# Gate weights loaded behind the fifth weight unit, gate rows read back behind the next unit, memory values stored two units later

## The chip, the cores and the metric

The kernel runs on one core of one Trainium2 chip. The metric is device microseconds of one execution of the whole program. The compared number is the median of the runs; the profile is one further execution.

## What is computed

The reference is one layer of a hybrid streaming encoder for 256 prompt tokens and 64 sample tokens (320 tokens, width 1024). Cut to what matters here:

```python
k = (rmsnorm(mem) @ w_mem_k); v = (rmsnorm(mem) @ w_mem_v)     # outputs mem_k_prompt, mem_v_prompt
z = rmsnorm(x) @ w_in                                          # 15 projections side by side
ig, lf = i_raw + i_b, log_sigmoid(f_raw + f_b)                 # the gates: 4 + 4 columns of w_in
bcum = cumsum(lf); m = max(...)                                # row maxima, outputs mlstm_m
w_intra = exp(dmat - m); w_inter = exp(inter - m)              # weights of the mLSTM heads
att = softmax(mq @ k.T) @ v                                    # attention into the memory tokens
x = x + (sum of three gated branches) @ w_out
x = x + hier_moe(rmsnorm(x))                                   # 32 experts, all weights streamed
```

All matrix products use a split of each float32 operand into a rounded high part and a rest, and three products of the parts.

## The kernel before, in words

The work is a list of steps, made once (`make_steps`), and every engine walks the list and does its own part of each step. The dense weights are cut into units of 1 MB, numbered from 0 in the order in which TensorE uses them: 0 to 3 are `w_mem_k`, 4 to 7 `w_mem_v` (each half of the contraction), 8 to 11 the query of the memory attention (`mq`), 12 to 19 the mLSTM queries and keys (`qk`), and so on. A unit goes through four hands:

1. SyncE (SP) issues its load (L711) into one of two raw slots (a third serves unit 2). From unit 3 on it waits first until VectorE has finished with the unit that held the slot (L707, semaphore `u_lo`): unit 3 waits for the rest of unit 0, unit 4 for that of unit 1, and unit n from 5 on for that of unit n-2.
2. ScalarE makes the high part (`unit_first_part`, L1228), after TensorE is done with the unit that held the rounded slot.
3. VectorE makes the rest (`unit_second_part`, L1634) and counts `u_lo`.
4. TensorE multiplies (L892 for `memk`, L827 for `memv`, L793 for `mq`, `qk` and others), after waiting for `u_lo`.

SP is one queue: what stands between two unit loads in the program delays the second. All its transfers run on the same 16 DMA engines. Before the change SP issues, around the places touched:

- ahead of unit 3: the three tiles of x (L702), then `load_gate_weights` (L618 to L625): two transfers of four columns of `w_in` each (1024 rows, 16 bytes of a row), two bias columns and the start maxima `m0c`. TensorE needs them for the step `gates`, which follows the first `memv` step of unit 4.
- behind unit 10: `spread_gate_rows` (L633 to L638) waits for the last exponential of the gate rows (`s_g4`), writes four rows to DRAM (L636), waits for that write (`s_rbw`), and reads them back, broadcast to 128 partitions (L638, 770 KB). VectorE waits for the read-back at its first `bc` step (L1733 to L1735).
- behind unit 11: `store_memory` (L640 to L648) stores the two `mlstm_m` outputs and then four halves of `mem_k_prompt` and `mem_v_prompt`.
- behind unit 13: a wait for all four of those stores, then the read of the prompt keys out of `mem_k_prompt` (L603, L610).

The order of steps at the read-back is `mq 0, bc 0, mq 1, (unit 10: high part and rest), bc 1, mq 2, ...`. Engine by engine: ScalarE evacuates `mq 0`, takes the exponential of `bc 0` (L1311, after VectorE's sum with the read-back rows), evacuates `mq 1` (L1321), and only then makes the high part of unit 10. VectorE does `bc 0`, then the rest of unit 10. TensorE does `mq 0` to `mq 3` from units 8 and 9 and then waits for unit 10.

The space of `memk` and `memv` is reused at the step `attention_done` (L1353, L1782, L2128), where three engines wait for all four stores.

Of the kernel before, what the change touches and what calls it, by code (L numbers as in the profile page):

```python
# [226 lines left out]
def unit_slot(n):  # L227

    return n if n < 3 else (n - 1) % RING
# [11 lines left out]
def build_kernel(nc, ins, outs):  # L241
    I, O = ins, outs
    ctx = ExitStack()
    with ctx:
# [3 lines left out]
        def sem(name):  # L248
            return ctx.enter_context(nc.semaphore(name))
# [56 lines left out]
        def take(*dims):  # L306
            v = at(off[0], *dims)
            off[0] += int(np.prod(dims))
            return v
# [9 lines left out]
        memk = take(2, D)  # L319
        memv = take(2, D)  # L320
# [148 lines left out]
        s_memout, s_cvout, s_cvs = sem("mem_out"), sem("conv_out"), sem("conv_rows")  # L469
# [44 lines left out]
        def done(*name):  # L514

            s = _by_name[name]
            return freed[s["ring"], s["eng"]], s["evacuated"]
# [29 lines left out]
        def _(sp):  # L547
            for r0, name in ((P_MIX, "norm_mix_g"), (P_MEM, "mem_norm_g")):
                sp.dma_start(prows[r0:r0 + 8, :], I[name][0, :].rearrange("(c p) -> c p", p=128)).then_inc(s_gains, 16)
            for i in range(2):  # L550
                sp.dma_start(mem_tm[:, i, :], I["mem_prompt"][0, i * 128:(i + 1) * 128, :]).then_inc(s_mem[i], 16)
                src = I["w_mem_k"][0, i * (D // 2):(i + 1) * (D // 2), 0:256].rearrange("(k p) n -> p k n", p=128)
# [48 lines left out]
            def load_key_blocks(dst, keys, signal):  # L601
                for a in range(4):
                    sp.dma_start(dst[32 * a:32 * a + 32, :].rearrange("i (b d) -> i b d", d=64),  # L603
                                 keys.rearrange("(b i) (a d) -> a i b d", i=32, d=64)[a]).then_inc(signal, 16)

            def load_cached_keys(h):
                load_key_blocks(cmk[:, h % 2, :], I["cache_mem_k"][0, 0, :, h, :], s_keys[h % 2])

            def load_prompt_keys(h):
                load_key_blocks(memk_b[:, h, :], O["mem_k_prompt"][0, 0, :, h, :], s_keys[h % 2])  # L610

            def load_cache_v(h):
                sp.dma_start(cmv[:, h % 2, :, :], I["cache_mem_v"][0, 0, :, h, :].rearrange("(j p) d -> p j d", p=128)).then_inc(s_cachev[h % 2], 16)

            def load_state(h):
                sp.dma_start(C0[:, h % 2, :, 0:HD], I["state_mlstm_C"][0, 0, h].rearrange("(k p) e -> p k e", p=128)).then_inc(s_c0[h % 2], 16)

            def load_gate_weights():  # L618

                sp.wait_ge(s_const, 3)  # L620
                for c0, col in ((0, I0), (32, F0)):
                    sp.dma_start(wif[:, :, c0:c0 + H], I["w_in"][0, :, col:col + H].rearrange("(k p) n -> p k n", p=128)).then_inc(s_par, 16)
                sp.dma_start(ib[:, :], I["mlstm_i_b"][0, :].rearrange("(h a) -> h a", a=1)).then_inc(s_par, 16)
                sp.dma_start(fb[:, :], I["mlstm_f_b"][0, :].rearrange("(h a) -> h a", a=1)).then_inc(s_par, 16)
                sp.dma_start(m0c[:, :], I["state_mlstm_m"][0, 0, :].rearrange("(h a) -> h a", a=1)).then_inc(s_par, 16)  # L625
            def load_router():
                sp.dma_start(bsb[:, :, :], I["gmlp_b_s"][0].partition_broadcast(128)).then_inc(s_bs, 16)
                sp.dma_start(wr[:, :, 0:G], I["w_router_group"][0].rearrange("(k p) n -> p k n", p=128)).then_inc(s_par3, 16)
                sp.dma_start(wr[:, :, G:G + E], I["w_router_expert"][0].rearrange("(k p) n -> p k n", p=128)).then_inc(s_par3, 16)
                sp.dma_start(wrb[:, 0:G], I["b_router_group"][0, :].partition_broadcast(128)).then_inc(s_par3, 16)  # L630
                sp.dma_start(wrb[:, G:G + E], I["b_router_expert"][0, :].partition_broadcast(128)).then_inc(s_par3, 16)

            def spread_gate_rows():  # L633

                sp.wait_ge(s_g4, 1)
                sp.dma_start(spread_rows, rb[0:H, :]).then_inc(s_rbw, 16)  # L636
                sp.wait_ge(s_rbw, 16)
                sp.dma_start(rbb[:, :, :].rearrange("p h t -> p (h t)"), spread_rows.rearrange("h t -> (h t)").partition_broadcast(128)).then_inc(s_rbb, 16)  # L638

            def store_memory():  # L640

                sp.wait_ge(s_g3, 1)
                sp.dma_start(O["mlstm_m_prompt"][0, 0, :].rearrange("(h a) -> h a", a=1), rows[0:H, R_MM, TP - 1:TP]).then_inc(s_mout, 16)
                sp.dma_start(O["mlstm_m_sample"][0, 0, :].rearrange("(h a) -> h a", a=1), rows[0:H, R_MM, T - 1:T]).then_inc(s_mout, 16)
                sp.wait_ge(*done("memv", 1, 1, 1))
                for name, src in (("mem_k_prompt", memk), ("mem_v_prompt", memv)):
                    for i in range(2):
                        sp.dma_start(O[name][0, 0, i * 128:(i + 1) * 128].rearrange("p h d -> p (h d)"), src[:, i, :]).then_inc(s_memout, 16)  # L648

            def store_conv():  # L650

                sp.wait_ge(*done("cvT", 1))
                for i, name in enumerate(("mlstm_conv_prompt", "mlstm_conv_sample")):
                    sp.dma_start(O[name][0, 0].rearrange("j (c p) -> (j c) p", p=128), cvs[:, i, :]).then_inc(s_cvout, 16)

            def keep_keys(h):

                sp.wait_ge(*done("kt", h, 0))
                sp.dma_start(k_store[:, h, :], kw[:, 0:2, :].rearrange("p i d -> p (i d)")).then_inc(s_kst, 16)
# [38 lines left out]
            for n, (name, col, *part) in enumerate(UNITS):  # L698
                if n == 3:
                    for i, (t0, rows_) in enumerate(TILES):  # L700
                        src = I["x_prompt"][0, t0:t0 + rows_, :] if i < 2 else I["x_sample"][0, :, :]
                        sp.dma_start(x_tm[0:rows_, i, :], src).then_inc(s_x, 16)  # L702
                    load_gate_weights()
                if n == 0:
                    continue
                if n >= 3:
                    sp.wait_ge(u_lo, n - 2 if n < 5 else n - 1)  # L707
                w = 512 if part else 256
                r0 = part[0] * 512 if part else 0
                src = I[name][0, r0:r0 + UW // w * 128, col:col + w].rearrange("(k p) n -> p k n", p=128)  # L710
                sp.dma_start(raw_unit[unit_slot(n)].rearrange("p (k n) -> p k n", n=w), src).then_inc(unit_full[unit_slot(n)], 16)  # L711
                if n == 6:
                    sp.dma_start(ws[:, :, :], I["gmlp_w_s"][0].rearrange("g t s -> t g s")).then_inc(s_ws, 16)
                elif n in (8, 9):
                    load_cached_keys(n - 8)
                    load_cache_v(n - 8)
                elif n == 10:
                    spread_gate_rows()
                elif n == 11:
                    store_memory()  # L720
                elif n == 13:
                    sp.wait_ge(s_memout, 64)
                    load_prompt_keys(0)
                    load_prompt_keys(1)
                elif n in (16, 18):
                    sp.wait_ge(s_kmT, n - 14)
                    load_cached_keys(n // 2 - 6)
                    load_prompt_keys(n // 2 - 6)
                elif n in (19, 21):
                    sp.wait_ge(*done("av", (n - 19) // 2, 1))  # L730
                    load_cache_v((n - 15) // 2)
                elif n == 23:
                    sp.wait_ge(*done("av", 3, 1))
                    load_state(0)
                    load_state(1)
                elif n == 24:
                    load_router()
                elif n == 26:
                    store_conv()
                elif n == 28:  # L740
                    keep_keys(0)
                    keep_values()
                elif n in (30, 33, 37, 40):
                    h = (30, 33, 37, 40).index(n)
                    store_state(h)
                    if h < 2:
                        load_state(h + 2)
                elif n in (31, 34, 38):
                    keep_keys((31, 34, 38).index(n) + 1)
                elif n == 43:  # L750
                    store_normalizer()
                elif n == 47:
                    store_gating_values()
                if n == len(UNITS) - 9:
                    load_unit(0, 0)
                elif n == len(UNITS) - 3:
                    load_unit(0, 1)
# [1482 lines left out]
```

## Time and profile before

| | |
|---|---|
| median of 3 runs | 840.59 us (840.16 to 841.1) |
| profiled execution | 841.19 us |
| its span in the trace | 839.4 us, 12162 instructions |
| TensorE busy | 823.4 us, 98% |
| VectorE, ScalarE, GpSimd busy | 586.7, 469.1, 62.8 us |
| DMA | 191.83 MB, mean 229 GB/s |
| granted TensorE clock | 0.998 |

The views used below are the page, the waits (who waited for whom, in total), the timeline (instructions in order of time, equal ones merged, with the idle time before the first of them in brackets and what ended it), the DMA issues (with the time from issue to landing), and windows of one microsecond each. "SPq" rows are issues of DMAs by SyncE; the second number is how long the issue took SyncE, not how long the transfer ran. A merged row that holds several issues spans the waits between them.

### The profile page before, as it was taken

The page shows a single profiled execution, that of the slowest core. Times are in us where ns is not written, and L with a number is a line of the kernel's source. Part 1 is how long each engine was busy: PE and PEld are TensorE (multiplying, and loading weights), DVE is VectorE, ACT ScalarE, POOL GpSimd, SP SyncE. Part 2 cuts the span into 40 slices and gives each one's busy share as a digit, 9 for nine tenths or more (in the row PEclk, how much of TensorE's full clock was granted, in tenths as well). Part 3 has the DMA queues.
Part 4 walks back from the last instruction along what each step waited for, and adds up shares of the span by engine and source line. Part 5 has one row for each costly group of instructions (what it writes and reads, how often), then busy time and mean ns, then how long its engine had stood idle before and what let it go on. Part 6 is the DMA issues. An engine that isn't in the chain of part 4 may idle for free. (4 is left out here: it accounts for less than half of the span.)

```text
span 839.4 us, 12162 instructions
## 1 busy us (share of the span) xinstructions
PE 823.4 (98%) x4744; PEld 732.3 (87%) x4744; DVE 586.7 (70%) x820; ACT 469.1 (56%) x622; POOL 62.8 (7%) x113
## 2 busy tenths in 40 slices
PE   7999999999999999999999999999999999999995
PEld 7979989988989998899999999878888888888884
DVE  5665487773445456695565456778989889889894
ACT  5645577754333324554333336656877768767773
POOL 1000100010000000000000000020004102210410
PEclk9999999999999999999999999999999999999999
DMA  8659855327534536345436467589999999999970
GB/s 269 208 142 291 221 142 132 118 81 220 165 126 126 176 115 199 126 151 163 152 110 216 151 201 256 209 264 409 389 357 351 358 397 381 352 373 366 382 279 18
DMA packets 111841, 191.83 MB, mean 229 GB/s; under 512 B 18692, under 2 KB 76960, under 8 KB 111648
## 3 DMA queue, kind: packets, MB, share of 16 engines
q1 hardware_dynamic: 109824, 185.91, 65.0%
q0 software_dynamic: 1152, 3.41, 1.1%
q10 hardware_dynamic: 800, 1.66, 0.6%
q8 instruction: 40, 0.66, 0.3%
q14 instruction: 25, 0.20, 0.1%
HBM read 181.70 MB, written 10.03 MB: 228 GB/s over the span
## 5 line engine op out<-in xcount | busy, mean ns | idle before, releaser
L1643 DVE TENSOR_TENSOR w_r<-arena,w_r 128x2048 fp32r<-128x2048 f32 x96 | 217.0, 2286 | 27.6 <-ACT w_r L1239 27.6
L1634 DVE TENSOR_TENSOR unit_r<-arena,unit_r 128x2048 fp32r<-128x2048 f32 x63 | 144.3, 2291 | 131.2 <-ACT unit_r L1228 131.1
L793 PE MATMUL pj<-xn_r,unit_r 128*128 128x320 f32 x1536 | 233.2, 311 | 0.8 <-issue 0.8
L793 PEld LDWEIGHTS pj<-xn_r,unit_r 128*128 128x128 f32 x1536 | 225.6, 188 | 4.7 <-issue 3.7
L1130 PE MATMUL pj<-w_r,xg 128*128 128x512 f32 x768 | 191.0, 398 | 0.5 <-DVE xg L1627 0.4
L1239 ACT ACTIVATE w_r<-arena 128x2048 fp32r<-128x2048 f32 x96 | 180.3, 1909 | 2.7 <-DMA arena<-in_w_exp_down 2.0
L1130 PEld LDWEIGHTS pj<-w_r,xg 128*128 128x128 f32 x768 | 141.8, 188 | 31.5 <-DVE xg L1627 0.8
L1228 ACT ACTIVATE unit_r<-arena 128x2048 fp32r<-128x2048 f32 x63 | 120.9, 1919 | 44.4 <-PE pj L793 23.6
L1159 PE MATMUL pj<-w_r,hidT 128*128 128x512 f32 x384 | 93.3, 392 | 0.6 <-ACT hidT L1490 0.6
L1159 PEld LDWEIGHTS pj<-w_r,hidT 128*128 128x128 f32 x384 | 71.8, 188 | 17.0 <-issue 0.8
L793 PE MATMUL pj<-br_r,unit_r 128*128 128x320 f32 x384 | 59.6, 311 | 0.0
L793 PEld LDWEIGHTS pj<-br_r,unit_r 128*128 128x128 f32 x384 | 56.7, 188 | 1.1 <-issue 1.1
L1490 ACT ACTIVATE hidT<-ms 128x256 fp32r<-128x256 f32 x32 | 12.3, 385 | 70.6 <-PE ms L1140 70.6
L827 PE MATMUL pj<-unit_r,xn_r 128*128 128x512 f32 x192 | 46.2, 394 | 0.0
L827 PEld LDWEIGHTS pj<-unit_r,xn_r 128*128 128x128 f32 x192 | 35.4, 188 | 7.7 <-issue 0.3
L1381 ACT ACTIVATE arena<-pj 128x320 f32<-128x320 f32 x24 | 10.4, 433 | 33.0 <-PE pj L793 33.0
L793 PE MATMUL pj<-u_r,unit_r 128*128 128x320 f32 x192 | 28.8, 309 | 0.0
L1650 DVE SCALAR_TENSOR_TENSOR arena<-arena,prT 128x323 f32<-128x323 f32 x48 | 27.3, 570 | 1.7
L793 PEld LDWEIGHTS pj<-u_r,unit_r 128*128 128x128 f32 x192 | 28.3, 188 | 0.0
L892 PE MATMUL pj<-unit_r,mn_r 128*128 128x256 f32 x192 | 24.3, 285 | 2.8 <-DVE unit_r L1638 1.7
L892 PEld LDWEIGHTS pj<-unit_r,mn_r 128*128 128x128 f32 x192 | 23.4, 191 | 3.4 <-issue 2.1
L915 PE MATMUL pj<-unit_r,mix_r 128*128 128x256 f32 x192 | 24.1, 283 | 0.1
(344 smaller groups left out, 793.3 us busy)
## 6 DMA issues: line engine op xcount, KB each, us to landing
arena<-in_w_in SPq DMA_DIRECT2D x40, 1024.0 KB, 5.5
arena<-in_w_exp_gate SPq DMA_DIRECT2D x64, 512.0 KB, 4.9
arena<-in_w_exp_up SPq DMA_DIRECT2D x64, 512.0 KB, 6.7
arena<-in_w_exp_down SPq DMA_DIRECT2D x64, 512.0 KB, 5.6
arena<-in_w_mem_v SPq DMA_DIRECT2D x4, 1024.0 KB, 5.3
arena<-in_w_br_mem SPq DMA_DIRECT2D x4, 1024.0 KB, 5.1
arena<-in_w_br_mlstm SPq DMA_DIRECT2D x4, 1024.0 KB, 5.1
arena<-in_w_br_gmlp SPq DMA_DIRECT2D x4, 1024.0 KB, 4.9
```

The lines of the kernel that those rows point to most:

```text
L793: last = mm(bank_of(s)[0:out_rows, 0:out_cols], l, r, start=k == 0, stop=k == len(pairs) - 1)
L827: last = mm(bank_of(s)[0:rows_, 0:512], l, r, start=kh + k + m == 0, stop=kh == 1 and k == 3 and m == passes - 1)
L892: last = mm(b[:, 0:256], mn_r[:, p, k, a[1] * 128:a[1] * 128 + 128], w[:, q, k, :], start=k + m == 0, stop=k == KC - 1 and m == 2)
L915: last = mm(b[0:n, 0:256], mix_r[:, p, k, t0:t0 + n], w[:, q, k, :], start=k + m == 0, stop=k == KC - 1 and m == 2)
L1130: last = mm(pj[:, x % 2, :].rearrange("p (h n) -> p h n", h=2), xg[g % 2][:, k0 + k, xp, :], w[:, wp, k, :, :], start=k0 + j == 0, stop=k0 ...
L1159: last = mm(pj[:, 2 + half, :], hidT[:, x % 2, xp, c, :], w_r[u % NS][:, wp, c * D + half * 512:c * D + half * 512 + 512], start=e == 0 an ...
L1228: af(unit_part(n, 0), raw_columns(n), ACT.Copy).then_inc(u_hi, 1)
L1239: af(w_r[u % NS][:, 0, :], raw_w[u % NS], ACT.Copy).then_inc(m_hi, 1)
L1490: af(hidT[:, x % 2, 0, :, :].rearrange("p a b -> p (a b)"), ms[:, x % 2, 0:DE], ACT.Copy).then_inc(m_hth, 1)
L1634: v.tensor_tensor(unit_part(n, 1), raw_columns(n), unit_part(n, 0), ALU.subtract).then_inc(u_lo, 1)
L1643: v.tensor_tensor(w_r[u % NS][:, 1, :], raw_w[u % NS], w_r[u % NS][:, 0, :], ALU.subtract).then_inc(m_lo, 1)
L1650: ins = v.scalar_tensor_tensor(o, r[:, j:j + CONVW], prT[:, P_CW + 16 * j + c:P_CW + 16 * j + c + 1], o, ALU.mult, ALU.add)
```

## The change

Three moves on SP's list; no computation changes.

- `load_gate_weights` goes from ahead of unit 3 to behind unit 4.
- The write of the gate rows stays behind unit 10; the wait for it and the read-back go behind unit 11. The stores of `mem_k_prompt` follow the read-back.
- The two `mlstm_m` stores go behind unit 12, the stores of `mem_v_prompt` behind unit 14. The read of the prompt keys behind unit 13 waits for the two key stores alone.

```diff
-            def spread_gate_rows():
+            def write_gate_rows():
                 sp.wait_ge(s_g4, 1)
                 sp.dma_start(spread_rows, rb[0:H, :]).then_inc(s_rbw, 16)
+            def spread_gate_rows():
                 sp.wait_ge(s_rbw, 16)
                 sp.dma_start(rbb[:, :, :].rearrange("p h t -> p (h t)"), spread_rows.rearrange("h t -> (h t)").partition_broadcast(128)).then_inc(s_rbb, 16)
...
-                    load_gate_weights()
                 if n == 0:
                     continue
...
-                if n == 6:
+                if n == 4:
+                    load_gate_weights()
+                elif n == 6:
...
                 elif n == 10:
+                    write_gate_rows()
+                elif n == 11:
                     spread_gate_rows()
-                elif n == 11:
-                    store_memory()
+                    store_memory("mem_k_prompt", memk)
+                elif n == 12:
+                    store_maxima()
                 elif n == 13:
-                    sp.wait_ge(s_memout, 64)
+                    sp.wait_ge(s_memout, 32)
                     load_prompt_keys(0)
                     load_prompt_keys(1)
+                elif n == 14:
+                    store_memory("mem_v_prompt", memv)
```

## Rows read from the trace of the kernel before

**Rows 1.** The page: busy time of engines.

```profile
PE 823.4 (98%) x4744; PEld 732.3 (87%) x4744; DVE 586.7 (70%) x820; ACT 469.1 (56%) x622; POOL 62.8 (7%) x113
```

**Rows 2.** Waits of TensorE, whole span: total us, times, longest.

```profile
PE pj L892 <- DVE unit_r L1634: 1.0, 1, 1.0
...
PE pj L793 <- issue: 0.8, 1, 0.8
```

**Rows 3.** Timeline, 0 to 70 us: start, duration (us), engine, line, operation.

```profile
11.86 4.52 SPq L622 DMA_DIRECT2D arena<-in_w_in  x2
12.26 1.22 DVE L1638 TENSOR_TENSOR unit_r<-arena,unit_r 128x1024 fp32r<-128x1024 f32 x1
...
21.62 1.06 ACT L1274 ACTIVATE arena<-arena 128x1024 f32<-128x1024 f32 x1 [0.68 <-DMA arena<-in_x_sample]
21.81 0.39 SPq L711 DMA_DIRECT2D arena<-in_w_mem_k  x1
...
24.67 0.19 ACT L1274 ACTIVATION_READ_ACCUMULATOR arena<-arena 64x1 f32 x1
...
26.87 1.91 ACT L1228 ACTIVATE unit_r<-arena 128x2048 fp32r<-128x2048 f32 x1 [2.01 <-DMA arena<-in_w_mem_k]
...
28.81 2.29 DVE L1634 TENSOR_TENSOR unit_r<-arena,unit_r 128x2048 fp32r<-128x2048 f32 x1 [3.57 <-ACT unit_r L1228]
...
31.25 3.11 PE L892 MATMUL pj<-unit_r,mn_r 128*128 128x256 f32 x24 [1.04 <-DVE unit_r L1634]
...
34.54 2.29 DVE L1634 TENSOR_TENSOR unit_r<-arena,unit_r 128x2048 fp32r<-128x2048 f32 x1
...
39.55 3.05 PE L827 MATMUL pj<-unit_r,mn_r 128*128 128x512 f32 x12
```

**Rows 4.** Windows of 1 us: engines, clock, DMA busy share, GB/s.

```profile
17.00:18.00 1.00, 1.00 (x10) 1.00 (x10) 0.99 (x2) 0.66 (x2) 0.00 (x0) 1.00 1.08 422
...
21.00:22.00 1.00, 1.00 (x11) 1.00 (x10) 1.00 (x1) 0.38 (x1) 0.00 (x0) 1.00 0.08 2
```

**Rows 5.** DMA issues near 22 us (units 3 and 4): KB, us to landing.

```profile
arena<-in_w_mem_k SPq DMA_DIRECT2D x1, 1024.0 KB, 5.0
arena<-in_w_mem_v SPq DMA_DIRECT2D x1, 1024.0 KB, 7.3
```

**Rows 6.** Timeline, 67 to 140 us, around the read-back.

```profile
69.70 2.29 DVE L1634 TENSOR_TENSOR unit_r<-arena,unit_r 128x2048 fp32r<-128x2048 f32 x1 [2.18 <-ACT unit_r L1228]
...
72.14 0.34 SPq L638 DMA_DIRECT2D arena<-gate_rows  x1
...
72.52 0.43 SPq L711 DMA_DIRECT2D arena<-in_w_in  x1
...
76.29 0.35 DVE L1735 TENSOR_SCALAR arena<-arena,cols 128x256 f32<-128x256 f32 x1 [3.30 <-DMA arena<-gate_rows]
...
77.93 2.06 ACT L1228 ACTIVATE unit_r<-arena 128x2048 fp32r<-128x2048 f32 x1
80.03 2.29 DVE L1634 TENSOR_TENSOR unit_r<-arena,unit_r 128x2048 fp32r<-128x2048 f32 x1 [2.86 <-ACT unit_r L1228]
...
82.42 21.35 PE L793 MATMUL pj<-xn_r,unit_r 128*128 128x320 f32 x144 [0.82 <-issue]
```

**Rows 7.** DMA issues at 66.8 us (unit 10), 72.1 us (read-back), 72.5 us (unit 11).

```profile
arena<-in_w_in SPq DMA_DIRECT2D x1, 1024.0 KB, 5.2
...
arena<-gate_rows SPq DMA_DIRECT2D x1, 770.0 KB, 4.1
...
arena<-in_w_in SPq DMA_DIRECT2D x1, 1024.0 KB, 8.2
```

**Rows 8.** Timeline, later: where unit 11 and unit 14 are first used, unit 14's issue.

```profile
84.74 2.06 ACT L1228 ACTIVATE unit_r<-arena 128x2048 fp32r<-128x2048 f32 x1
...
95.25 17.33 SPq L711 DMA_DIRECT2D arena<-in_w_in  x3
...
107.69 1.91 ACT L1228 ACTIVATE unit_r<-arena 128x2048 fp32r<-128x2048 f32 x1
```

More of the change, by code:

```diff
@@ L631, in load_router, with store_maxima @@
                 sp.dma_start(wrb[:, G:G + E], I["b_router_expert"][0, :].partition_broadcast(128)).then_inc(s_par3, 16)
-            def spread_gate_rows():
+            def write_gate_rows():
                 sp.wait_ge(s_g4, 1)
                 sp.dma_start(spread_rows, rb[0:H, :]).then_inc(s_rbw, 16)
+            def spread_gate_rows():
                 sp.wait_ge(s_rbw, 16)
                 sp.dma_start(rbb[:, :, :].rearrange("p h t -> p (h t)"), spread_rows.rearrange("h t -> (h t)").partition_broadcast(128)).then_inc(s_rbb, 16)
-            def store_memory():
+            def store_maxima():
                 sp.wait_ge(s_g3, 1)
@@ L644, in store_memory @@
                 sp.dma_start(O["mlstm_m_sample"][0, 0, :].rearrange("(h a) -> h a", a=1), rows[0:H, R_MM, T - 1:T]).then_inc(s_mout, 16)
+            def store_memory(name, src):
                 sp.wait_ge(*done("memv", 1, 1, 1))
-                for name, src in (("mem_k_prompt", memk), ("mem_v_prompt", memv)):
-                    for i in range(2):
-                        sp.dma_start(O[name][0, 0, i * 128:(i + 1) * 128].rearrange("p h d -> p (h d)"), src[:, i, :]).then_inc(s_memout, 16)
+                for i in range(2):
+                    sp.dma_start(O[name][0, 0, i * 128:(i + 1) * 128].rearrange("p h d -> p (h d)"), src[:, i, :]).then_inc(s_memout, 16)
             def store_conv():
```

## The prediction

> **What bounds the kernel now.** I read the page first. TensorE is busy for 98% of the span and the next engine for 70% [rows 1], so in the end only time in which TensorE stands still, or starts standing still, counts. VectorE, ScalarE and the DMA engines matter where TensorE waits for them. So the second view is the list of TensorE's own waits. Two of its entries concern the places that the change touches: 1.0 us at the first multiplication of unit 3, ended by VectorE's rest, and 0.8 us in the projection at L793, put down to "issue" [rows 2]. Everything else that the change moves lies beside running matmuls. The third view is the timeline around these two gaps, which says what was really late.
>
> *First gap, at 31.25 us* [rows 3]. TensorE could have gone on at 31.25 - 1.04 = 30.21 us. Read it backwards: VectorE's rest of unit 3 ran from 28.81 to 31.10, ScalarE's high part from 26.87, and that one had waited 2.01 us for the load. The load was issued at 21.81, although its slot was free at 12.26 + 1.22 = 13.48. In between SP was issuing the gate weights and small columns, from 11.86 on. In that time the DMA engines ran dry: full at 17 to 18 us (422 GB/s), idle at 21 to 22 us (2 GB/s) [rows 4]. So SP's queue, not bandwidth, made unit 3 late.
>
> *Second gap, at 82.42 us* [rows 6]. TensorE could have gone on at 81.60. VectorE's rest of unit 10 ended at 80.03 + 2.29 = 82.32. It had waited for ScalarE (77.93 on), and ScalarE came to unit 10 only behind the first `bc` step, which VectorE began at 76.29 after 3.30 us of waiting for the read-back of the gate rows. The read-back was issued at 72.14 and took 4.1 us [rows 7]. So here the chain is: read-back landed, 76.29; then 6.1 us of VectorE, ScalarE, ScalarE, VectorE in a fixed order; then TensorE. Any delay of the read-back is a delay of TensorE, one for one, because 0.82 us of stall is already there. That is the main point of this forecast.
>
> **Part 1, gate weights behind unit 4.** Removed from ahead of unit 3: five issues, from 11.86 to 21.81. Unit 3 is now issued at about 13.5, right behind x in the queue. What does it cost to transfer? Units 3 and 4 were issued at 21.81 and 22.25 and landed 5.0 and 7.3 us later [rows 3, 5], at 26.81 and 29.55: a megabyte behind a megabyte adds 2.74 us (unit 4's issue is the next thing SP does, 0.44 us later). Behind x, which landed no later than 21.62, unit 3 therefore lands by 24.4. ScalarE is busy with the squares of x until 24.67 + 0.19 = 24.86, so it starts the high part there or earlier, not at 26.87: a gain of 2.0 us for VectorE, which ends at about 29.1. TensorE needs it at 30.21. The stall of 1.04 us goes whole, with 1.1 us to spare. If the transfer turned out up to 1.1 us slower, nothing changes; if x and unit 3 shared the bandwidth so badly that it was 2 us slower, the gain would be near zero. What is late next: unit 4's rest, at 34.54 + 2.29 = 36.83, used at 39.55 [rows 3], 2.7 us of room, so a shift of 1.04 is covered.
>
> The five issues now stand behind unit 4's load, whose slot is free once the rest of unit 1 is done, so they start at about 18 us. They took 9.95 us before (11.86 to 21.81), so SP is free at about 28.5. Queued behind them is unit 5, which must wait for the rest of unit 3 (29.1 in the new run) anyway. The gate weights themselves are needed behind the first step of `memv`, 39.55 + 3.05 - 1.04 = 41.6 us. They have some 13 us of cover; without it the cost would be the 10 us of issue. I take -1.04, with bounds -1.2 and 0.
>
> **Part 2, the read-back behind unit 11.** SP issued the read-back at 72.14 and unit 11 at 72.52. Unit 11's own condition, the rest of unit 9, was met at 69.70 + 2.29 = 71.99 [rows 6]. In the changed kernel unit 11 goes out at 72.0 and the read-back at about 72.4: SP's wait for the write ends at about the same moment as before, so its removal from in front of unit 11 is worth 0.5 us to a load that ScalarE takes up only at 84.74, 12 us later [rows 8]. That gain is nil on TensorE's path.
>
> The cost is the read-back's place in the queue. It now has 1 MB in front of it. By units 3 and 4 a transfer issued just behind another one lands later by its own size at the same rate: 2.74 us per 1024 KB, so 770 KB add 2.06. Unit 11 would land at 72.0 + 5.2 (unit 10's time [rows 7]) = 77.2, and the read-back at 79.3. Before it was there at 76.24. So it is 3.0 us late. Bounds: a lower one is 2.4, if the queue moves at the 422 GB/s of [rows 4] (1.05 MB / 422 GB/s = 2.5, with unit 11 0.15 us ahead of the old read-back). The upper one comes from unit 11 itself, which took 8.2 us behind the read-back and in front of the stores, landing at 80.7, 4.5 us after it instead of 2.7 [rows 7]. The two key stores now follow the read-back at once, and if they slow it in that proportion, 770 KB take 3.4 and it lands at 80.6, 4.4 us late. I take 3.0, since the sum by units 3 and 4 is two loads in a row, as here, and the stores are behind it.
>
> The Trainium skill, DMA: Bandwidth & Descriptors, "Anatomy of one DMA", gives a fixed part of about 2 us and bytes over 436 GB/s for the rest. By it the megabyte ahead would cost an estimated 2.4 us and not 3.0, and the whole change would come out 0.6 us better than below, at 842.0. The trace's own step from unit 3 to unit 4, 2.74 us per megabyte [rows 5], is slower than that, and the sum goes by the trace.
>
> TensorE's stall at `mq 4` grows from 0.82 to 3.8 us: all of the delay goes through, as shown above. What follows is ordered by TensorE again: unit 11's parts wait for `mq` to free slots, unit 12's load waits for the rest of unit 11. None of it is nearer to an absolute time, so nothing is won back.
>
> **Part 3, stores.** `mlstm_m` (two issues) behind unit 12, `mem_v_prompt` (two issues, 1 MB) behind unit 14, the wait for stores at unit 13 now for two. Behind unit 14 (issued at 95.25, taken up by ScalarE at 107.69 [rows 8]) some 3 us of stores in the queue fit into the room even if they delayed that unit wholly. Their finish is needed only at the end of attention, far behind. Their going away from 74 to 77 us relieves unit 11, which had 4 us of room already (landed 80.7, used 84.74). I cost this part at 0, with bounds -0.3 and +0.3.
>
> **Sum.** -1.04 + 3.0 + 0 = +2.0 us. The profiled execution took 841.19 and would take 843.2; it lies 0.6 above the median of the runs. Against the median, 840.59 + 2.0 = 842.6. Its own bounds: 840.59 - 1.2 + 2.4 - 0.3 = 841.5, and 840.59 + 0 + 4.4 + 0.3 = 845.3 if every part goes badly.
>
> **Rivals.**
>
> *A. The read-back is not held up by the unit in front* (0.20). If the engines work on both transfers at once, the later and smaller one may land nearly as early: delay 0 to 1, total 839.6 to 840.6, not slower. The place is the DMA queue at 72 us, and the point from which it decides is a delay of 1.04 us, where both parts cancel. For it speaks that the transfers are issued only 0.4 us apart. Against it speaks that unit 4, issued 0.44 us behind unit 3, landed 2.74 us behind it [rows 5], and that before the change unit 11, 0.38 us behind the read-back, did not keep it from landing in 4.1 us.
>
> *B. TensorE's clock falls in the longer gap* (0.12). The gap grows from 0.82 to 3.8 us; the granted clock reads 1.00 in every window read here, the 2.4 GHz level [rows 4], and no gap of such a length is in the trace. If TensorE came back at 1.2 GHz, 320 columns would take 267 ns each. Now 24 such matmuls take 21.35 / 6 = 3.56 us, 148 ns each [rows 6]. So a group of 24 costs 2.8 us more. Half a group to a whole one: 844.0 to 845.4. The Trainium skill, TensorE: Matmul & The Clock Gate, "Part 1: The HAM clock gate", says that an idle array falls to half its clock and regains it after sustained work; the trace of before has no row to weigh that against.
>
> *C. Unit 3 lands no earlier in use* (0.08). Then only part 2 counts: 843.6. Against it stands the idle stretch of the DMA engines at 21 us [rows 4].
>
> *D. The order makes no difference* (0.05): both stalls stay as they are, 840.6. *E. A gain from the stores that I don't see* (0.05): under 838.9.
>
> **How the numbers follow.** The main case has 0.50, with 842.6 and 841.5 to 845.3. Predicted is 842.6. The range 839.7 to 845.0 takes in the main case, C, D, nearly all of A and half of B, and leaves out about 1 in 8. The cases on both sides of no change hold most of the chance, so the main case's own range stands above. A measurement of this kernel can tell about 0.2% from no change, 1.7 us: faster means under 838.9, slower over 842.3. Slower: four fifths of the main case, since most of its span lies above 842.3 (0.40), B 0.12 and C 0.08: 0.60. Faster: E and a tenth of A, 0.07. Same: the rest, 0.33.
>
> **What the profile of the changed kernel would show.** For part 1: unit 3's load issued near 13.5 us, no TensorE wait at L892 for L1634, the DMA engines not idle at 21 us, and the gate weights issued between 18 and 28 us. For part 2: the read-back's issue directly behind unit 11's, its landing time well above 4.1 us (6.9 by the sum), VectorE's wait for `gate_rows` near 6.3 us instead of 3.3, and TensorE's gap before `mq 4` near 3.8 us. For part 3: unit 14's high part without a wait for its load. B would show a granted clock under 1.00 behind that gap. The forecast is wrong if the read-back lands within 5 us of its issue, or if `mq 4` starts less than 1 us later, after the shift of part 1, than it did.

## The result and the profile after

The changed kernel takes 845.9 us (median of 6 runs, 845.73 to 847.08); the kernel before, run beside it, 840.85 (840.05 to 842.34). The ratio is 1.0061, 95% interval 1.0048 to 1.0074. It is slower, as forecast, but by 5.05 us and not by 2.0, and it lies outside the range. Below, medians are set against those of the kernel before in the same comparison, which were 840.25 to 840.59 in the later ones.

The page of the changed kernel, engines and clock, to be laid beside [rows 1]. The fifth slice of the clock line reads 8:

```profile
PE 825.9 (98%) x4744; PEld 735.3 (87%) x4744; DVE 586.8 (70%) x820; ACT 469.3 (56%) x622; POOL 62.6 (7%) x113
...
PEclk9999899999999999999999999999999999999998
```

TensorE's waits, against [rows 2]. The wait at unit 3 (L892 for L1634 before, L904 for L1646 now) is gone, and what is left at L904 is for another line; the one "by issue" at the projection (L793 before, L805 now) has gone from 0.8 to 4.8 us:

```profile
PE pj L805 <- issue: 4.8, 1, 4.8
PE pj L904 <- DVE unit_r L1650: 1.8, 2, 1.3
```

The timeline at the front, against [rows 3]. Unit 3 is issued at 13.36, ScalarE comes from the squares of x straight to its high part, and the gate weights are issued from 18.07 on:

```profile
13.36 0.39 SPq L716 DMA_DIRECT2D arena<-in_w_mem_k  x1
...
18.07 4.70 SPq L622 DMA_DIRECT2D arena<-in_w_in  x2
...
24.41 0.19 ACT L1286 ACTIVATION_READ_ACCUMULATOR arena<-arena 64x1 f32 x1
24.51 1.90 ACT L1240 ACTIVATE unit_r<-arena 128x2048 fp32r<-128x2048 f32 x1
...
26.43 2.29 DVE L1646 TENSOR_TENSOR unit_r<-arena,unit_r 128x2048 fp32r<-128x2048 f32 x1 [1.44 <-ACT unit_r L1240]
```

The timeline at the read-back, against [rows 6]:

```profile
65.78 14.34 PE L805 MATMUL pj<-xn_r,unit_r 128*128 128x320 f32 x96
...
70.43 0.37 SPq L716 DMA_DIRECT2D arena<-in_w_in  x1
...
70.84 0.58 SPq L642 DMA_DIRECT2D arena<-gate_rows  x1
71.47 1.07 SPq L654 DMA_DIRECT2D out_mem_k_prompt<-arena  x2
78.89 0.35 DVE L1747 TENSOR_SCALAR arena<-arena,cols 128x256 f32<-128x256 f32 x1 [7.48 <-DMA arena<-gate_rows]
...
80.52 2.01 ACT L1240 ACTIVATE unit_r<-arena 128x2048 fp32r<-128x2048 f32 x1
82.56 2.29 DVE L1646 TENSOR_TENSOR unit_r<-arena,unit_r 128x2048 fp32r<-128x2048 f32 x1 [2.81 <-ACT unit_r L1240]
...
84.95 23.60 PE L805 MATMUL pj<-xn_r,unit_r 128*128 128x320 f32 x144 [4.83 <-issue]
```

The chain is the one of before, step for step: read-back, VectorE, ScalarE, VectorE, TensorE. The read-back landed 7.9 us after its issue (DMA issues, against [rows 7], where it took 4.1):

```profile
out_mem_k_prompt<-arena SPq DMA_DIRECT2D x2, 512.0 KB, 9.8
arena<-gate_rows SPq DMA_DIRECT2D x1, 770.0 KB, 7.9
```

The fifth `mq` step starts at 84.95 and not at 82.42, 2.5 us later. That is the gap's growth of 4.0 us less 1.5 us by which TensorE came to it earlier (80.12 and not 81.60).

The last line of the timeline shows the second loss: 144 matmuls took 23.60 us, where the same 144 took 21.35 [rows 6]. The windows of 1 us (engines' busy time, then granted clock, DMA share, GB/s) say why:

```profile
80.00:81.00 1.00, 0.12 (x1) 0.00 (x0) 0.00 (x0) 1.00 (x4) 0.64 (x3) 1.00 0.24 86
...
83.00:84.00 1.00, 0.00 (x0) 0.00 (x0) 1.00 (x1) 0.00 (x0) 0.00 (x0) 0.55 0.00 0
...
86.00:87.00 1.00, 1.00 (x6) 1.00 (x5) 0.41 (x4) 1.00 (x6) 0.73 (x3) 0.50 0.80 180
...
89.00:90.00 1.00, 1.00 (x6) 1.00 (x5) 0.61 (x1) 0.35 (x1) 0.00 (x0) 0.54 0.35 117
90.00:91.00 1.00, 1.00 (x9) 1.00 (x8) 1.00 (x1) 0.00 (x0) 0.00 (x0) 1.00 0.00 0
```

TensorE's last matmul ended at 80.12. The clock fell from 2.4 to 1.2 GHz about 3 us later, and TensorE came back at 84.95 to half speed, 5 or 6 matmuls in a microsecond instead of 9, until close to 90 us.

### The profile page after: what moved, and what is told of

Its sections match the earlier page's. It is cut to its first block, busy times and chain, and to the rows that moved or that the text cites. A ratio compares the mean times of both kernels' runs of the same rounds, so it can differ in the third digit from the quotient of the medians.

```text
span 843.9 us, 12162 instructions
## 1 busy us (share of the span) xinstructions
PE 825.9 (98%) x4744; PEld 735.3 (87%) x4744; DVE 586.8 (70%) x820; ACT 469.3 (56%) x622; POOL 62.6 (7%) x113
## 4 chain that ended last, share of the span: by engine, by line
PE 93%; DVE 2%; DMA 2%; ACT 2%; issue 1%; POOL 0%; SPq 0%; POOLq 0%; DVEq 0%; ACTq 0%
PE pj L805 36%; PE pj L1142 21%; PE pj L1171 10%; PE pj L839 8%; PE pj L927 3%; PE pj L904 3%; PE ms L973 1%; PE ms L992 1%; PE pj L846 1%; DMA arena<-gate_rows 1%; DMA arena<-in_w_in 1%; PE ms L1152 1%; PE ms L1008 1%; ACT unit_r L1240 1%; PE ms L861 1%
## 5 line engine op out<-in xcount | busy, mean ns | idle before, releaser
L805 PE MATMUL pj<-xn_r,unit_r 128*128 128x320 f32 x1536 | 235.5, 313 | 4.8 <-issue 4.8
L805 PEld LDWEIGHTS pj<-xn_r,unit_r 128*128 128x128 f32 x1536 | 227.8, 190 | 8.8 <-issue 7.7
L1646 DVE TENSOR_TENSOR unit_r<-arena,unit_r 128x2048 fp32r<-128x2048 f32 x63 | 144.3, 2290 | 130.7 <-ACT unit_r L1240 130.7
L805 PE MATMUL pj<-br_r,unit_r 128*128 128x320 f32 x384 | 59.6, 311 | 0.0
L805 PEld LDWEIGHTS pj<-br_r,unit_r 128*128 128x128 f32 x384 | 56.7, 188 | 1.1 <-issue 1.1
L805 PE MATMUL pj<-u_r,unit_r 128*128 128x320 f32 x192 | 28.8, 309 | 0.0
L805 PEld LDWEIGHTS pj<-u_r,unit_r 128*128 128x128 f32 x192 | 28.3, 188 | 0.0
L904 PE MATMUL pj<-unit_r,mn_r 128*128 128x256 f32 x192 | 24.1, 285 | 1.8 <-DVE unit_r L1650 1.8
L904 PEld LDWEIGHTS pj<-unit_r,mn_r 128*128 128x128 f32 x192 | 23.3, 191 | 2.3 <-issue 2.2
```

The costliest lines, as they stand in the source:

```text
L805: last = mm(bank_of(s)[0:out_rows, 0:out_cols], l, r, start=k == 0, stop=k == len(pairs) - 1)
L904: last = mm(b[:, 0:256], mn_r[:, p, k, a[1] * 128:a[1] * 128 + 128], w[:, q, k, :], start=k + m == 0, stop=k == KC - 1 and m == 2)
L1646: v.tensor_tensor(unit_part(n, 1), raw_columns(n), unit_part(n, 0), ALU.subtract).then_inc(u_lo, 1)
```

## The experiments

Theory: the whole loss is the read-back's place in the queue, paid twice, once as a longer gap and once as half a clock. The main rival is that the other two moves cost something too, or that the two losses aren't what they seem.

**Undo part 2 only.** The read-back is again directly behind its write:

```diff
                     write_gate_rows()
-                elif n == 11:
                     spread_gate_rows()
+                elif n == 11:
                     store_memory("mem_k_prompt", memk)
```

> The changed kernel with the read-back of the gate rows put back directly behind its write, ahead of unit 11; gate weights behind unit 4 and the later stores stay. Theory (the whole loss is the read-back's place: 4.0 us of delay and 2.25 us of halved clock): TensorE's gap before the fifth mq step is 0.8 us again, the clock stays at 1.00, and the time is 1.2 to 1.5 us under the kernel before, about 839.5. Rival (the gate weights' new place or the stores also cost something): at or above the kernel before, 840.9 or more.

Measured: 839.85 us, ratio 0.9995 (0.9986 to 1.0004). The gap is 0.9 us, the clock 1.00. The whole loss of the change goes with this one move. The gain against the kernel before is only 0.4 us and not told from nothing; 1.2 to 1.5 were expected. TensorE's waits of this kernel:

```profile
PE pj L805 <- issue: 0.9, 1, 0.9
```

**Undo part 1 only.** `load_gate_weights` back ahead of unit 3:

```diff
                         sp.dma_start(x_tm[0:rows_, i, :], src).then_inc(s_x, 16)
+                    load_gate_weights()
...
-                if n == 4:
-                    load_gate_weights()
-                elif n == 6:
+                if n == 6:
```

> The changed kernel with the gate weights back ahead of unit 3; only the read-back's place and the stores are changed against the kernel before. Theory: the two parts are independent, so this is the changed kernel plus the 1.2 to 1.5 us that the front gave: 847.2, with the wait of 1.0 us at unit 3 back and the gap of 4.8 us and the half clock as they are. Rival (moving the gate weights is what lengthened the wait for the read-back): clearly under the changed kernel's 845.9.

Measured: 845.9 us, ratio 1.0062 (1.0048 to 1.0075), no worse than the changed kernel. The read-back took 8.2 us, the gap was 5.0 us, and the clock fell. Here the theory missed as the forecast did: the wait at unit 3 did not come back. The timeline of this kernel's SP shows the unit out at 20.33, not at 21.81:

```profile
11.63 4.15 SPq L622 DMA_DIRECT2D arena<-in_w_in  x2
15.83 3.79 SPq L623 DMA_DIRECT2D ib<-in_mlstm_i_b  x1
...
20.33 0.67 SPq L717 DMA_DIRECT2D arena<-in_w_mem_k  x1
```

The same issues took 9.95 us of SP in the profiled execution of the kernel before and 8.7 here, for the same work. TensorE's stretch from the first to the second of these rows is 9.10 us, against 10.20 in the kernel before (the third and fourth row) and 8.93 in the changed one (23.81 to 32.74):

```profile
23.91 0.27 PE L950 MATMUL ms<-ident,arena 56*128 56x56 f32 x1
...
33.01 1.04 PE L932 MATMUL ms<-ident,arena 128*128 128x128 f32 x8
```

```profile
24.00 0.27 PE L939 MATMUL ms<-ident,arena 56*128 56x56 f32 x1
...
34.20 1.04 PE L921 MATMUL ms<-ident,arena 128*128 128x128 f32 x8
```

So unit 3 cost about 0.2 us here, and 1.3, of which 1.0 is the wait itself, in the execution on which the forecast rests.

**Part 1 alone**, on the kernel before (`load_gate_weights` behind unit 4, as in the change, nothing else).

> The kernel before with the gate weights behind unit 4, nothing else. By the record of the prediction -1.04 us. Theory now (the profiled execution of before had a longer wait at unit 3 than most; where the gate weights stood ahead of unit 3 in another run, that wait was 0.3 us): 0.3 to 0.5 us under the kernel before. Rival (the whole 1.0 us in each execution): 1.0 us or more under it.

Measured: 839.88 against 840.59, a ratio of 0.9994 (0.9985 to 1.0003). That is 0.7 us under it, where 0.3 to 0.5 were expected. The interval runs from a gain of 1.3 us to a loss of 0.3, so it shuts out neither zero nor the forecast's 1.04: that the move is worth less than 1.0 in most executions rests on three traces, not on this time.

**Part 3 alone** (`mlstm_m` and `mem_v_prompt` stored later, read-back and gate weights in the places of before).

> The kernel before with the stores alone moved: mlstm_m behind unit 12, mem_v_prompt behind unit 14, the prompt keys waiting for the two key stores. Theory (they lie beside running matmuls in either place): no difference, within 0.3 us of the kernel before, TensorE's gap 0.8 us. Rival (the stores slow the transfers that TensorE waits for): 0.5 us or more off, either way.

Measured: 840.45 against 840.59, ratio 1.0001 (0.9992 to 1.0010). Nothing, as forecast. Its trace gives one more sample of both gaps with gate weights and read-back in their old places, 0.4 and 1.2 us:

```profile
29.90 3.11 PE L903 MATMUL pj<-unit_r,mn_r 128*128 128x256 f32 x24 [0.40 <-DVE unit_r L1645]
...
81.38 21.36 PE L804 MATMUL pj<-xn_r,unit_r 128*128 128x320 f32 x144 [1.15 <-issue]
```

**Fill the gap, leave the wait.** TensorE gets work that changes nothing ahead of its wait for unit 10:

```diff
                     n = s["unit"]
+                    if kind == "mq" and a[0] == 4:
+                        for _ in range(14):
+                            mm(b[:, 0:128], ident[:, :], ident[:, :], start=True, stop=True)
                     if n:
                         pe.wait_ge(u_lo, n + 1)
```

> The changed kernel with 14 small matmuls on the identity, whose result is overwritten, put ahead of TensorE's wait for unit 10 (8 of them took 2.08 us in the trace of before, so 3.6 us of the 4.8 us gap are filled). The wait for unit 10 itself is untouched. Theory (the clock fell because TensorE stood still): granted clock 1.00 throughout, the time 2.25 us under the changed kernel, 843.6. Rival (the half clock costs nothing on the path, or falls for another reason): 845.9, as the changed kernel.

Measured: 844.04 us, ratio 1.0040 (1.0027 to 1.0053), 1.9 us under the changed kernel with more instructions in it. Each set against the kernel before beside it, it is 3.8 us over, and the changed kernel 5.05 and, run again, 5.8. In the profiled execution the clock stayed at 1.00 and the 144 matmuls took 21.39 us:

```profile
80.63 3.29 PE L880 MATMUL pj<-ident 128*128 128x128 f32 x28
85.77 21.39 PE L805 MATMUL pj<-xn_r,unit_r 128*128 128x320 f32 x144 [1.86 <-DVE unit_r L1649]
```

The wait for unit 10, from 80.63 to 85.77, is no shorter than before (5.1 against 4.8 us); only the standing still is. So half a clock is a price of its own, of about 2 us, on top of the gap.

**Take the key stores from behind the read-back.**

```diff
                 elif n == 11:
                     spread_gate_rows()
-                    store_memory("mem_k_prompt", memk)
                 elif n == 12:
+                    store_memory("mem_k_prompt", memk)
                     store_maxima()
```

> The changed kernel with the two stores of mem_k_prompt behind unit 12 instead of directly behind the read-back. Theory (the stores behind the read-back slowed it by 1.0 us against two loads in a row): it lands 7.0 us after its issue instead of 8.0, the gap is 3.8 us; 844.9 if the clock still falls, 842.6 if it doesn't. Rival (the whole delay is the unit in front): landing 8.0 us, 845.9.

Measured: 844.33 us, ratio 1.0040 (1.0026 to 1.0054). The read-back took 6.8 us instead of 7.9 and the gap was 3.8 us; in the profiled execution the clock still fell.

```profile
arena<-gate_rows SPq DMA_DIRECT2D x1, 770.0 KB, 6.8
```

```profile
84.57 23.57 PE L805 MATMUL pj<-xn_r,unit_r 128*128 128x320 f32 x144 [3.83 <-issue]
```

So the delay has two parts: 6.8 - 4.1 = 2.7 us for the megabyte in front, and 7.9 - 6.8 = 1.1 us for the stores behind. The two runs below that also have the key stores behind unit 12 show 6.8 again; every trace with the read-back behind unit 11 and the key stores directly behind it shows 7.9 or 8.2. The theory expected 844.9 if the clock fell; two of the five executions have mean clocks of 0.996, above all of the changed kernel's, so it may not have fallen in these.

**Both savings together**, 14 matmuls in that kernel.

> The kernel with the key stores behind unit 12, and 14 small matmuls ahead of TensorE's wait for unit 10, so that about 0.5 us of its gap of 3.8 us is left unfilled. Theory (two terms that add: the key stores behind the read-back, 1.1 us, and the halved clock, 2.2 us): 845.9 - 1.1 - 2.2 = 842.6, clock at 1.00. Rival (the two savings are one and the same): 844.0, as each of them alone.

Measured: 842.43 us, ratio 1.0026 (1.0016 to 1.0036), 3.6 us under the changed kernel beside it (846.04), where the two terms make 3.3. The clock stayed at 1.00 and the 144 matmuls took 21.38 us. The two terms add.

**A gap between.** The same with 5 matmuls.

> The kernel with the key stores behind unit 12 (its gap was 3.8 us, the clock fell, 844.3), with 5 small matmuls on the identity ahead of TensorE's wait for unit 10: 14 of them took 3.29 us, so 5 leave about 2.7 us of standing still. Question: does the clock fall in a gap of this length? If it falls as in the gap of 3.8 us: 844.3. If it stays at 1.00: 842.3. The kernel before, with its gap of 0.8 us, kept it; a run with 1.9 us left kept it too.

Measured: 844.08 us, ratio 1.0038 (1.0024 to 1.0051). In the profiled execution TensorE stood still for 2.69 us, and the clock fell just after it had come back, as the windows below the timeline row show; the 144 matmuls took 22.91 us:

```profile
83.86 22.91 PE L805 MATMUL pj<-xn_r,unit_r 128*128 128x320 f32 x144 [2.69 <-DVE unit_r L1649]
```

```profile
83.00:84.00 1.00, 0.14 (x1) 0.14 (x2) 1.00 (x3) 0.00 (x0) 0.00 (x0) 1.00 0.00 0
84.00:85.00 1.00, 1.00 (x7) 1.00 (x8) 1.00 (x8) 0.55 (x2) 0.00 (x0) 0.97 0.12 17
85.00:86.00 1.00, 1.00 (x6) 1.00 (x5) 0.37 (x4) 1.00 (x5) 0.74 (x3) 0.50 0.80 162
```

The five executions don't agree: mean clocks of 0.994, 0.994 and 0.996 go with 844.1 to 844.2 us, and two of 0.998 with 842.4 and 843.0. Only one of these executions, of 844.08 us, has a trace, and it shows the fall. A mean of 0.996 tells little by itself, since the kernel before has it in executions from 839.2 to 841.4 us; the two of 0.998 are at the 842.3 expected without a fall, or not far from it. So by the times the clock seems to fall in some executions at this length and not in others; no trace shows one in which it stayed.

**The changed kernel again**, beside these two.

> The changed kernel as it is, once more, beside the two runs above on the same chip: 845.9 by its earlier runs, the clock at half behind the gap of 4.8 us. If its gap or its clock differ from the first trace, the sizes of the terms read there are those of one execution only.

Measured: 846.04 us, ratio 1.0064 (1.0050 to 1.0078). The gap is 4.83 us as in the first trace, the read-back took 7.9 us, the 144 matmuls 23.73. The sizes of these terms are not those of one execution only.

**Untie the chain.** In the changed kernel, each `bc` step stands two `mq` steps later:

```diff
-            if c < H:
-                step("bc", c, ring=None, eng=None)
+            if 2 <= c < 2 + H:
+                step("bc", c - 2, ring=None, eng=None)
```

> The changed kernel with each bc step (the first work on the read-back rows) two mq steps later in the list, so that neither ScalarE nor VectorE waits for the read-back ahead of unit 10. Theory (the read-back reaches TensorE only through the order mq 0, bc 0, mq 1, unit 10): the read-back still lands about 8 us after its issue, but TensorE's gap ahead of the fifth mq step goes whole, the 0.8 us of before too, and the clock stays at 1.00: 845.9 - 4.8 - 2.25 = 838.9. Rival (unit 10 itself or unit 11 is late, and the wait moves to the next unit): 841 to 845.

Measured: 838.67 us, ratio 0.9977 (0.9968 to 0.9986): faster than both kernels. The read-back is as late as ever, and nobody on TensorE's path waits for it. The 96 and the 144 matmuls have become one stretch of 240 with no gap:

```profile
arena<-gate_rows SPq DMA_DIRECT2D x1, 770.0 KB, 7.9
```

```profile
66.09 35.46 PE L805 MATMUL pj<-xn_r,unit_r 128*128 128x320 f32 x240
```

**The same with the read-back first again.**

> As the run with the bc steps two later, and the read-back directly behind its write as in the kernel before. Theory: with nothing waiting for it, the read-back's place is worth nothing: the same time as that run, 838.9. Rival (the read-back's early place helps or hurts unit 11 or something later): a difference of more than 0.5 us between the two.

Measured: 838.73 us, ratio 0.9981 (0.9972 to 0.9990), 0.06 us from the other. With nothing waiting for it, the place of the read-back is worth nothing. This shows the mechanism from the other side: the place cost what it did only through the order `mq 0, bc 0, mq 1, unit 10`.

## Why the prediction was wrong in size

*What bounds the kernel, and the chain at the read-back.* Right. The delay of the read-back came through to TensorE, and with the `bc` steps moved it did not.

*Part 1, -1.04 us.* The mechanism was right: issued at 13.36, wait gone. Its size was that of one execution. It was taken from one wait in one trace, and that execution (841.19 us) was slower than most. With the gate weights in the old place the wait at unit 3 was 1.0, about 0.2 and 0.4 us in three traces. The medians give 0.4 (with the stores moved too) and 0.7 us, with intervals that take in both zero and 1.04, so its size in a median stays open. The lower bound of zero covered it, but the gap between the profiled execution and the median, which the prediction noted as 0.6 us, should have been read as a sign that a wait in it might be an untypical one. The forecast added the same delta to the median instead.

*Part 2, +3.0 us.* The term for the megabyte in front was right: 6.9 us from issue to landing by the forecast's sum, 6.8 measured with no stores behind. The sum took its step of 2.74 us from unit 3 to unit 4, and the issue of unit 4 at 22.25, on which it rests, is this row of the kernel before:

```profile
22.25 14.98 SPq L711 DMA_DIRECT2D arena<-in_w_mem_v  x3
```

The choice not to count the stores behind was the mistake. The prediction had the row that showed it, unit 11's 8.2 us in front of stores [rows 7], worked out 4.4 us from it, and kept that as the upper bound, on the ground that the stores are behind. They cost 1.1 us all the same. The gap grew from 0.8 to 4.8, by 4.0: the 3.8 us of longer landing, and some 0.2 for the later issue.

*Rival B, the clock.* This is the step that failed: the clock's fall was left out of the sum, with a chance of 0.12, and it happened in all four profiled executions with a gap of 3.8 us or more. Its price, 1.4 to 2.8 us, was met: 23.60 - 21.35 = 2.25, and 1.9 by the medians. In part that is luck, since the forecast had no row for its "half a group to a whole one". The trace of before had no row on the fall either, the longest wait of TensorE in it being 1.6 us, and "no row" was taken for "unlikely". Either of the two missed terms alone would have left the forecast within its range, which ended at 845.0 (842.6 + 1.1 = 843.7, 842.6 + 2.25 = 844.9). The rule of the Trainium skill, TensorE: Matmul & The Clock Gate, "Part 1: The HAM clock gate", that an idle array falls to half its clock, agrees with the traces here: it fell in or behind gaps of 5.0, 4.8, 3.8 and 2.7 us, and in no trace at one of 1.9 or less.

*The Trainium skill's estimate*, 2.4 us for the megabyte in front (DMA: Bandwidth & Descriptors, "Anatomy of one DMA"): measured 2.7. That section of the Trainium skill is on transfers issued from GpSimd, and these are issued by SyncE, which the prediction left out. The trace's own step was the nearer one.

*Rival A, the read-back isn't held up.* Wrong, 7.9 against 4.1 us. *Rivals C, D, E:* none came about. *Part 3:* nothing, as forecast.

The sum with measured terms: -0.5 (part 1, between the 0.4 and the 0.7), +4.0 (gap), +2.25 (clock), 0: +5.75 us. Between the two profiled executions alone the first term is -1.5, and the sum 4.8; they took 841.19 and 845.73 us, 4.5 apart. The two comparisons of the changed kernel with the kernel before gave 5.05 (845.9 against 840.85) and 5.8 (846.04 against 840.25). The difference between these two is within the spread of the runs of before. The gap with the read-back in its old place was 0.8, 0.9, 1.1 and 1.2 us in four traces, which moves the sum by 0.4.

## What to carry to other kernels

Before moving a transfer behind another, find who waits for it and whether that engine is already late; if it is, as here, the transfer in front is paid in full, and the transfers behind it may cost too. A stall of TensorE that grows by some microseconds can be paid twice, since the clock may halve in it: give this a chance by the length of the gap, not by whether the trace of before has such a gap. And where a wait on a late transfer sits in the middle of an engine's order, moving the consumer in the list can be worth more than moving the transfer: here 838.7 us against 839.9 with the transfer back behind its write.

## What the runs showed of the hardware

- A load of 770 KB with 1 MB of loads 0.4 us ahead of it took 6.8 us in three traces, and 7.9 to 8.2 in five when 1 MB of stores was issued 0.6 us behind it; with nothing in front and 1 MB of loads 0.4 us behind it, it took 4.1 to 4.4 in five. So stores issued later slowed a load issued before them. The windows from 75 to 78 us of the changed kernel show 297, 222 and 314 GB/s, and those from 75 to 77 us of the kernel with the key stores behind unit 12 show 425 and 408. Why is not settled.
- The granted clock fell 3.0 us after the last matmul in the changed kernel, and in the kernel with the key stores behind unit 12 already about 2 us after it (its last matmul ended at 80.74, and the window from 82 to 83 us reads 0.83). In both it stayed at 1.2 GHz through about the first 5 us of work after the gap. In the kernel with 5 small matmuls and a gap of 2.69 us it fell only 1.1 us after TensorE had come back.
- Small matmuls on the identity, 14 in 3.29 us, kept the clock up through a wait that still left 1.9 us idle.
